# A transformer step on one core: router logits taken from the turned residual stream, token modulation on GpSimd

## What is computed

```
def _layer(x, cvec, p, kv_ctx):
    ...
    x = x + g1 * mix                                  # mix = merged @ w_out
    h2 = _rms_norm(x, p['norm2_g']) * (1 + sc2) + sh2
    x = x + g2 * _expert_choice_ffn(h2, p)

def _expert_choice_ffn(h, p):                         # 16 experts
    cap = CAPACITY_FACTOR * S // N_EXPERTS            # 64 sample and 16 prompt tokens for each expert
    logits = h @ p['w_router'] + p['b_router']
    aff = softmax(logits)
    gate, idx = lax.top_k(aff.transpose(0, 2, 1), cap)
    xs = h[idx]
    y = (silu(xs @ w_gate) * (xs @ w_up)) @ w_down * gate      # for each expert, added at idx
```

## Time and profile before

| what | value |
|---|---|
| median of 3 runs | 1402.83 us (1402.35 to 1403.17) |
| the profiled execution's own time | 1399.74 us |
| its span in the profile | 1397.9 us |
| mean granted TensorE clock | 0.946 |
| TensorE (PE) busy | 1262.8 us, 90% |
| VectorE (DVE) busy | 914.3 us, 65% |
| ScalarE (ACT) busy | 619.3 us, 44% |
| GpSimd (POOL) busy | 300.6 us, 22% |
| DMA | 302.54 MB, mean 216 GB/s |

### The profile page before, as it was taken

The page is one execution under the profiler, slowest core; times in us unless marked ns, Lnnn a source line. Parts: engine busy times, 40 slices in busy tenths (PEclk is TensorE's granted clock), DMA queues, the critical chain, the costliest instruction groups (busy, mean ns, idle before and its releaser), DMA issues.

```text
span 1397.9 us, 18848 instructions
## 1 busy us (share of the span) xinstructions
PE 1262.8 (90%) x7338; PEld 1009.5 (72%) x7338; DVE 914.3 (65%) x1070; ACT 619.3 (44%) x693; POOL 300.6 (22%) x199
## 2 busy tenths in 40 slices
PE   2899979997999999999798459999999999999992
PEld 1688769985888999999797436666666666666661
DVE  1501656779766233613745549999999999999993
ACT  2421122221433222231212237777777777777772
POOL 1051000000332222233221402222222222222212
PEclk9899989997999999999998569999999999999996
DMA  9764651321110111235202969999999999999964
GB/s 282 247 211 151 226 91 61 106 70 60 44 48 28 43 53 60 90 104 199 63 31 109 380 214 352 379 378 378 380 381 378 380 381 382 381 381 381 381 232 160
DMA packets 156070, 302.54 MB, mean 216 GB/s; under 512 B 6984, under 2 KB 60707, under 8 KB 155758
## 3 DMA queue, kind: packets, MB, share of 16 engines
q1 hardware_dynamic: 144268, 267.63, 53.4%
q10 hardware_dynamic: 7986, 21.66, 4.2%
q0 software_dynamic: 3760, 12.45, 4.2%
HBM read 286.63 MB, written 15.08 MB: 216 GB/s over the span
## 4 chain that ended last, share of the span: by engine, by line
PE 82%; DVE 10%; ACT 2%; DMA 2%; issue 2%; SPq 1%; POOL 0%; ACTq 0%; POOLq 0%; DVEq 0%
PE bank L1287 16%; PE bank L1288 15%; PE bank L1289 15%; PE bank L1310 5%; PE bank L1311 4%; PE bank L1312 4%; PE bank L1313 4%; PE bank L1314 4%; PE bank L1315 4%; DVE fa L913 2%; PE bank L1516 1%; PE bank L1589 1%; PE bank L1342 1%; PE bank L1489 1%; DMA mask<-const_mask 1%
## 5 line engine op out<-in xcount | busy, mean ns | idle before, releaser
L1219 DVE TENSOR_TENSOR l2r<-w,h2r 128x2048 fp32r<-128x2048 f32 x189 | 431.6, 2290 | 55.2 <-ACT h2r L820 53.5
L820 ACT CAST h2r<-w 128x2048 fp32r<-128x2048 f32 x192 | 367.1, 1913 | 132.0 <-PE bank L1289 128.1
L1287 PE MATMUL bank<-h2r,xTh 128*80 128x512 f32 x512 | 203.4, 397 | 1.0 <-DVE xTl L1225 1.0
L1288 PE MATMUL bank<-l2r,xTh 128*80 128x512 f32 x512 | 202.1, 395 | 0.0
L1289 PE MATMUL bank<-h2r,xTl 128*80 128x512 f32 x512 | 200.6, 392 | 0.0
L495 POOL TENSOR_TENSOR half<-half 1x1 f32<-1x1 f32 x32 | 67.6, 2112 | 369.2 <-DVE ye L1263 367.9
L441 POOL TENSOR_TENSOR lring<-wring,hring 128x2048 fp32r<-128x2048 f32 x21 | 96.9, 4614 | 196.9 <-ACT hring L536 196.9
L1310 PE MATMUL bank<-hTh,hring 128*128 128x320 f32 x320 | 107.0, 334 | 3.3 <-DVE hTl L974 3.3
L1289 PEld LDWEIGHTS bank<-h2r,xTl 128*80 128x80 f32 x512 | 76.2, 149 | 43.1 <-issue 0.9
L1287 PEld LDWEIGHTS bank<-h2r,xTh 128*80 128x80 f32 x512 | 76.2, 149 | 42.6 <-DVE xTl L1225 1.3
L1288 PEld LDWEIGHTS bank<-l2r,xTh 128*80 128x80 f32 x512 | 76.3, 149 | 39.8 <-issue 0.7
(11 more groups left out here) (276 smaller groups left out, 2455.8 us busy)
## 6 DMA issues: line engine op xcount, KB each, us to landing
w<-in_w_e_gate SPq DMA_DIRECT2D x64, 1024.0 KB, 12.0
w<-in_w_e_up SPq DMA_DIRECT2D x64, 1024.0 KB, 12.7
w<-in_w_e_down SPq DMA_DIRECT2D x64, 1024.0 KB, 12.2
wring<-in_w_in SPq DMA_DIRECT2D x21, 1024.0 KB, 5.2
fa<-in_w_ada SPq DMA_DIRECT2D x13, 1024.0 KB, 7.4
wring<-in_w_ada SPq DMA_DIRECT2D x11, 1024.0 KB, 7.6
wring<-in_w_out SPq DMA_DIRECT2D x4, 1024.0 KB, 5.3
fa<-in_w_in SPq DMA_DIRECT2D x3, 1024.0 KB, 5.1
```

The source lines that it names most:

```text
L820: act.copy(h2r[:, k % 3, :], w2[:, k, :]).then_inc(e_hi, 1)
L1219: dve.tensor_tensor(l2r[:, k % 3, :], w2[:, k, :], h2r[:, k % 3, :].bitcast(F32), ALU.subtract).then_inc(e_lo, 1)
L1287: pe.matmul(out, lh, rh, start=start, stop=False)
L1288: pe.matmul(out, lh, rl, start=False, stop=False)
```

## The change

1. **Logits from the residual stream.** Since the norm's factor is one number for each token, the logits of a token are (its `X2` row times a router matrix scaled by (1 + sc2) * norm2_g) times that factor, plus a bias row (sh2 times the router matrix, plus b_router). The scaled matrices `wr2` (one for the prompt, one for the samples) and the bias rows `lb` are made in the first three quarters: five small DMAs bring scale, shift and gain as 40 rows (`rows40`), TensorE turns them once, VectorE makes `a2c` and `wr2`, TensorE makes the bias rows in eight narrow matmuls and spreads them in two.
2. **Half of it during the third quarter.** `turn_x2(k, i)` turns four 128-column chunks of a tile of `X2`, `route(k, i)` makes four matmuls with them. Half 0 needs only quarters 0 and 1 and runs between the tile products of quarter 2; half 1 runs between those of quarter 3. ScalarE copies the turned halves 0 out of PSUM, VectorE the halves 1 (`turned`).
3. **One softmax for four tiles.** The four sample tiles' logits stand in one PSUM bank, and the softmax is made for all of them in seven VectorE instructions and one exponential. The prompt tile's product, its turning and its softmax come after, between the rounds of `top`.
4. **Modulated tokens on GpSimd.** VectorE makes them for the first tile alone. For the other four ScalarE multiplies by the norm's factor (`normalise`) and GpSimd multiplies by `A2bc` and adds `sh2bc` (`modulate`). `h2t` has four buffers.
5. **Weights and their low parts.** The memory of the expert stage is laid out anew, so SP loads the first two units after quarter 2, seven after quarter 3 and the last three when the stores and turns that used their place are done. The low parts of the first three units move from GpSimd to VectorE, behind the choice.

```diff
@@ sync
-            unit_used(sp, N_U - 1)
...
+                    elif k == 0:
+                        unit_used(sp, N_U - 2)
+                    elif k == 2:
+                        unit_used(sp, N_U - 1)
+                    elif k == 9:
+                        sp.wait_ge(s_hst[3], 16)
+                        sp.wait_ge(s_xst, 16 * TT)
+                        sp.wait_ge(s_t2, 2 * TT)
+                        sp.wait_ge(s_hx, TT - 1)
@@ gpsimd
-            for k in range(3):
-                gp.wait_ge(e_hi, k + 1)
-                gp.tensor_tensor(l2r[:, k, :], w2[:, k, :], h2r[:, k, :].bitcast(F32), ALU.subtract).then_inc(e_lo, 1)
+            def modulate(i):
+                g = 0 if TILE_ORDER[i] == 0 else 1
+                gp.wait_ge(s_hx, i)
+                gp.tensor_tensor(h2t[i % 4], h2t[i % 4], A2bc[:, g, :], ALU.mult).then_inc(s_nm, 1)
+                gp.wait_ge(s_nm, i)
+                gp.tensor_tensor(h2t[i % 4], h2t[i % 4], sh2bc[:, g, :], ALU.add).then_inc(s_h2p, 1)
+            gp.wait_ge(s_a2, 2)
+            for i in range(4):
+                rstd2(i)
+            gp.wait_ge(s_aff, 1)
+            modulate(1)
+            rstd2(4)
+            for i in range(2, TT):
+                modulate(i)
             gp.wait_ge(s_route, 2)
-            for st in (s_hst[0], s_hst[1], s_xst):
...
+            for b in range(4):
+                gp.wait_ge(s_hst[b], 32 if b == 0 else 16)
@@ scalar
+            normalise(2)
+            normalise(3)
+            softmax_exp(0)
+            store_x(3)
+            act.wait_ge(s_q2, 4)
+            sum_squares(4)
+            store_x(4)
+            normalise(4)
+            for i in range(1, 4):
+                store_h(i)
+                e_hi_unit(0, i - 1)
+            store_h(4)
+            softmax_exp(1)
+            act.dma_start(fgbc, a["final_norm_g"].rearrange("(o d) -> o d", o=1).to_broadcast([P, D])).then_inc(s_fg, 16)
+            act.dma_start(g2r[0:CAP_S, :], mods_d[1:2, 3 * D:4 * D].to_broadcast([CAP_S, D])).then_inc(s_g2, 16)
@@ vector
+            top(NP, T, 0, CAP_S, {0: lambda: residual(3, TILE_ORDER[4]), 1: lambda: turned(4), 4: lambda: softmax(1, 0),
+                                  5: lambda: softmax(1, 1), 6: prompt_affinity})
             top(0, NP, CAP_S, CAP_P)
...
             dve.wait_ge(s_route, 2)
             dve.wait_ge(s_g2, 32)
...
+            dve.wait_ge(s_h2p, 4)
+            dve.wait_ge(s_hst[2], 16)
+            dve.wait_ge(s_hst[3], 16)
+            for k in range(3):
+                e_lo_unit(0, k)
             x_lo(0)
-            dve.wait_ge(e_lo, 3)
@@ tensor
+            u = out_unit(2)
+            for m, t in enumerate(TILE_ORDER):
+                token_major("out", 2, t, u)
...
+                turn_x2(0, m)
+                if m >= 1:
+                    route(0, m - 1)
+            u = out_unit(3)
+            for m in range(4):
+                token_major("out", 3, TILE_ORDER[m], u)
+                if m == 0:
+                    route(0, 4)
+                if m >= 1:
+                    turn_x2(1, m - 1)
                 if m >= 2:
...
+                    route(1, m - 2)
+            turn_x2(1, 3)
+            route(1, 2)
+            route(1, 3)
+            token_major("out", 3, TILE_ORDER[4], u)
+            pe.wait_ge(s_aff, 1)
```

More of the change, by code:

```diff
@@ L1194, in top @@
+            turned(1)
+            residual(3, TILE_ORDER[3])
+            turned(2)
+            turned(3)
+            softmax(0, 0)
+            softmax(0, 1)
+            def top(x0, x1, v0, cap, between={}):
                 for r in range(cap // 8):
```

321 lines of the change are left out of this document (193 added, 128 removed).

## The result

| | before | after | |
|---|---|---|---|
| median of 4 runs, us | 1402.59 (1395.00 to 1403.17) | 1377.90 (1374.66 to 1380.04) | ratio 0.9836 [0.9812, 0.9860] |
| profiled execution, us | 1399.74 | 1380.04 | -19.7 |
| its span, us | 1397.9 | 1378.2 | -19.7 |

The forecast was a median of 1388.8 in a range from 1384.5, and -14.0 between profiled executions. It was too cautious: -19.7 between the profiled ones, -24.7 between the medians. On a second chip the medians lay 18.1 us apart (1381.54 against 1399.60).

The account below looks back on a forecast made before the run. TensorE bounds the experts, so only their start can move: gates -14.6 us plus 0.6 handing over makes -14.0, 1385.7 us profiled. Adding 3.1 gives a median of 1388.8, range 1384.5 to 1398.0.

Parts of the forecast that it names:

- the pacemaker: End of the choice: GpSimd's last modulated tile, at 787.4, sets when the gates are out, at 796.9 instead of 811.5.
- handing over: Allowance for some ten new places between engines, 0.06 us each, adding 0.6 us to the sum.
- the price of narrow work: TensorE's inserted half-turns at 0.55 us and half-logits at 0.98 us, five of each 7.6 us.
- the step to the median: From the profiled execution's 1385.7 us, 3.1 us added as in the kernel before, giving a median of 1388.8.
- The clock allowance: Fourth quarter: half a tile product at TensorE's lower clock level, +1.3 us, between 0 and 1.7.
- GpSimd's passes: Modulation on GpSimd: 2.41 us for a pass of 1024 columns, from a straight line, bounds 2.31 and 3.03.
- The two adds of the prompt's softmax: During the choice: VectorE adds with both inputs in SBUF wait for GpSimd, at 2.4 us each.
- The held gather: Rival behind the gates: VectorE's low parts start first and hold GpSimd's gather; +6.6 us, median 1395.4, chance 0.32.
- held for one instruction: Rival behind the gates: the shared port holds GpSimd for one whole instruction only; +2.3 us, median 1391.1, chance 0.06.
- The clock rival: Quarters 3 and 4: narrow logits pull TensorE to 1.2 GHz and keep it there; +17 us, 1419.8, chance 0.05.
- slower GpSimd: Rival in modulation: passes at 3.03 us, six in the chain 3.7 us longer; median 1392.5, chance 0.10.
- not what it says: Rival: gather bound otherwise, modulated tokens or last weights too late, half the gain goes; 1396, chance 0.03.

Follow-up runs that it names:

- after_again: The changed kernel run once more with no edit; ratio to the kernel before 0.9872, median 1381.54 us.
- tile_g2r_guard: Changed kernel with g2r issued early, VectorE's low parts waiting for GpSimd's step, and VectorE modulating the second tile in quarter 4; ratio 0.9821 to before.
- mod_before: Changed kernel with the sample tiles' modulation back on VectorE ahead of the choice, GpSimd keeping the prompt tile; ratio 0.9908 to before.
- wait_mod: mod_before plus TensorE's second half-turn of each sample tile waiting for that tile's modulated tokens; ratio 1.0018 to the kernel before.
- late_half: Changed kernel with the five first half-turns and four half-logits in one block behind quarter 3's products; ratio 0.9888 to before.
- extra_pass: Changed kernel with one more GpSimd pass of 128x1024 ahead of the fourth sample tile's modulation; ratio 0.9908 to before.
- g2r_early: Changed kernel with the two g2r transfers issued before the store of the third modulated tile; ratio 0.9892 to before.
- weights_late: Changed kernel with the first two expert weight units waiting for the out product's last unit; ratio 0.9854 to before.
- exp_first: Changed kernel with the prompt's exponential ahead of the last modulated tile's store in ScalarE's program; ratio 0.9846 to before.

## Why the prediction was too small

The direction, the chain of four engines and the pacemaker were right. The forecast median was 10.9 us too high. Of this 5.7 us lie between the profiled executions (19.7 - 14.0), and 5.2 in the step from there to the median: the forecast added 3.1 us because the median of before lay that far above its profiled execution, and the median of the changed kernel lay 2.1 below its own (1377.9 against 1380.0).

The 5.7 us add up, to rounding, step by step. The forecast's 742.9 for the start of quarter 4 counts all five first half-turns with their half-logits; the mark q4, the last residual of quarter 3, comes before the last such pair of 1.5 us, so the forecast for this mark is 741.4.

| step of the forecast | forecast, us | measured, us | missed, us |
|---|---|---|---|
| the mark q4 comes later | +7.1 | +6.1 | 1.0 |
| q4 to the affinities (741.4 to 764.3) | 22.9 | 21.1 | 1.8 |
| affinities to the copy | 2.4 | 1.4 | 1.0 |
| copy to the last modulated tile | 20.7 | 20.2 | 0.5 |
| last tile to the gates | 9.5 | 9.2 | 0.3 |
| gates to the first expert matmul, against before | 0 | +1.0 | -1.0 |
| experts and tail, against before | 0 | -1.4 | 1.4 |
| handing over | +0.6 | no row shows it | 0.6 |

- **The first term that failed** is the price of narrow work, "half a turn is 0.55, half the logits 0.98 us". I halved the shown length of whole groups in the earlier trace rows. In the profile after a half-turn is shown as 0.60 and half-logits as 0.96, but the logits begin 0.16 us before the turn is shown to end, and two residuals with both between them lie 4.21 us apart instead of 2.88:

```profile
736.19 0.42 DVE L1211 SCALAR_TENSOR_TENSOR xg_f<-bank,fa 128x256 f32<-128x256 f32 x1 [3.32 <-PE bank L1393]
```

```profile
735.99 0.60 PE L1682 MATMUL bank<-ident,fa 128*128 128x128 f32 x4
736.43 0.96 PE L1694 MATMUL bank<-fa 128*128 128x16 f32 x8
...
740.20 0.60 PE L1682 MATMUL bank<-ident,fa 128*128 128x128 f32 x4
```

From 736.19 to the 740.40 of the first rows above, that is 1.33 us for the pair and not 1.53. All narrow work of quarters 3 and 4 up to the logits was forecast at 13.97 us; it took 5.10 up to q4 and, with four products of 2.88 us taken off the 19.06 us from 740.40 to 759.46, 7.54 behind it: 1.3 us less. The bias work before quarter 3 took 1.1 instead of 1.8, the softmax 2.0 instead of 2.5, and the 0.4 for handing over in quarter 4 did not show. Against these 2.9 us stands a slip of 0.2: the terms of the first sum, 6.7 + 0.3 + 0.3 + 1.5, make 8.8 and not 8.6.
- **The second** is the step to the median. That a kernel's median lies above its profiled execution by what it did before was taken from the kernel before, and no run here shows that it carries over; in after_again the median was the profiled execution's own time, 1381.5.
- **Experts and tail** were said to keep their length. The 1.4 us that they gave are within what these stages differ by from run to run (548.8 to 550.1 us for the experts, 25.7 to 27.1 behind their last matmul), so they are luck and not the change. The way from the gates to the first expert matmul, said to stay, was 1.0 us longer: TensorE waited 0.6 us more for the gather (8.6 against 8.0), and the low parts, which began late because VectorE waited 3.5 us for g2r, ended last.
- **The clock allowance** of 1.3 us was not needed: level 1.00 up to 764. The risk was real. tile_g2r_guard lost 1.5 us in just this product without any gap before it, mod_before and wait_mod lost the level behind gaps, late_half behind a block of narrow work.
- **GpSimd's passes** took 2.34 to 2.36 us where the straight line gave 2.41; six of them in the chain are the 0.4 us. That its last tile sets the gates stands by extra_pass, us for us. What its pacing costs, 4.5 us, stands by mod_before; 2.8 of them went in tile_g2r_guard.
- **The two adds of the prompt's softmax** were forecast to wait for GpSimd at 2.4 us each; 1.82 and 2.07 were seen. The prompt's residual ran free, as forecast.
- **The held gather** did not happen in the changed kernel, but the margin given for it, half a microsecond, was wrong: g2r landed 11 us after its issue and not 8, and VectorE began 3.6 us behind the gates; in extra_pass, with the same order of issues, it landed after 7.2 and the gather was held. The price, up to 6.6, was right in size: 4.9 to 6.3 us in five kernels. So it was a rival with the right mechanism whose condition I had judged too finely from one landing time; that the changed kernel escaped it was the luck of a late landing. The other rival, held for one instruction at +2.3, is right for each access, but there are three of them, one behind the other.
- **The handing over** of 0.6 us was an allowance without a row, and no row after shows it. The low parts, which I had beside the gather's flight, end last: the first expert matmul waited 1.33 us for VectorE.
- **The clock rival, slower GpSimd and "not what it says"** have nothing for them in the trace of the changed kernel. In the price of the clock rival, nine half-turns of 0.55 us at half speed would add 5.0 and not 3.5.

Most allowances pointed one way, and each was small. But together they were enough: with the measured -19.7 in place of -14.0 and the same step to the median the forecast would have been 1383.1, already below the range.

The rest, to the median, is likely not the kernel's change. The executions of before lie at 1395.0 and at 1402.4 to 1403.2, those of after at 1374.7 and 1376.2 and at 1379.6 and 1380.0. TensorE at the beginning of the changed kernel and of extra_pass, which do the same there:

```profile
26.20 0.29 PE L1477 MATMUL bank<-ident,fa 20*128 20x20 f32 x1 [16.53 <-DMA mask<-const_mask]
```

```profile
21.66 0.29 PE L1480 MATMUL bank<-ident,fa 20*128 20x20 f32 x1 [11.82 <-DMA mask<-const_mask]
```

The first loads took 4.5 us longer in one of them, and the first residual of the out product came at 693.8 and 689.4. All milestones behind it, counted from there, agree to 0.1 us between kernels. Only profiled executions have a trace, so how much of the way from 19.7 to 24.7 this is, and what makes the loads differ, stays open.

## What to carry to other kernels

Price work that is inserted into a running stream by the distance between two milestones with and without it, not by the shown length of its group. When a chain is freed of a step, ask what the waiting engine's gaps cost it beside their length: of the 19.2 us that wait_mod gave back, 12.2 were gaps and some 7 the clock behind them. And when two engines share a port, a small instruction in front of a long transfer must be let through by order: making something ready earlier, as g2r here, cost 5 us until VectorE was made to wait for GpSimd's step.

## What the runs showed that was not expected

- VectorE's long instructions hold three small GpSimd accesses one after the other, also the issue of the indirect gather: 2.91 us instead of 1.07. VectorE's MAX8, FIND_INDEX8 and MATCH_REPLACE8 ran at their 0.66 to 0.68 us through all GpSimd passes, as did copies out of PSUM; only its additions with both inputs in SBUF were held (1.8 to 2.1 us instead of 0.17, and 1.82 instead of 0.42).
- The landing of g2r, a broadcast in two transfers of 256 and 64 KB, took 7.2 us (extra_pass), 8.0 (g2r_early), 9.5 (weights_late) or 11 (the changed kernel, exp_first, late_half) after its issue, with the DMA engines full of weights. The hold of the gather hangs on it.
- The granted level fell at the end of a block of five half-turns and four half-logits, although TensorE was 94% busy in 4 us of it (3.76 of 4.00), and did not fall when the same instructions stood between tile products. In the fifth product of quarter 4 it held in the changed kernel and fell in tile_g2r_guard, behind the same TensorE instructions without a wait.
